# Dense weight blocks laid out by the host, and the inputs read by channels

## The chip, the cores and the metric

The kernel runs on one NeuronCore of a Trainium2 chip. The metric is the device time of one execution in microseconds. TensorE (PE) multiplies and turns, VectorE (DVE) and ScalarE (ACT) work on tiles, GpSimd (POOL) takes small powers and builds masks, SyncE (SP) issues most of the transfers (DMA). Everything is float32; a product is made of three rounded ones.

## The reference

Two transformer blocks run one after the other on x (256 tokens, 1024 channels). The first has a mixer (differential attention and a gated linear attention), cross attention to a memory `mem`, and a mixture of 32 experts of which each token takes two. The second has three attention branches, one of them cross attention to `mem_2`, gates and an output product. Every block starts with a norm over the channels and a product with a weight matrix:

```
u = rmsnorm(h) * norm_g
p = u @ w_in                       # parts: dq, dk, dv, gq, gk, gv, gg, gr
...
kv = (rmsnorm(mem) * norm_m) @ w_kv
...
kv2 = (rmsnorm(mem_2) * g_mem) @ w_mem_kv
```

The norm's row factor is one number for each token, `rsqrt(mean(x*x) + eps)`; the gain is one number for each channel.

## The kernel before

The dense products work on blocks of 1024 rows by 512 columns of weights, 40 of them, in a written order (`FIRST_BLOCKS`, 18 before the experts, `SECOND_BLOCKS`, 22 behind them). A block comes in two halves of 1 MB. `load_dense` on SP's queue loads a half into one of four buffers of the ring (`raw_half`), once the half that was there is used. From `block_cols` a half is four pieces of 512 floats, 2 KB, in each partition. ScalarE rounds the half into its hi part (`split_hi`, L898), VectorE subtracts to get the lo part in place (`split_lo`, L1418), and TensorE makes three products for each pair of tiles (`dense`, L2362 to L2364): hi by hi, hi by lo, lo by hi. With `moving` the weights stream past the inputs (512 columns a product), with `standing` the weights stand (256 columns).

The inputs must be by channels, split in the same way. x, mem and mem_2 come with tokens in partitions. ScalarE squares and sums the rows (`square_row`, `square_rows`), VectorE makes the mean, POOL the power (L784), VectorE scales the rows (`scale_rows`, L1371), TensorE turns them (`turn_normed`, 16 transposes of 128x128, L2299), and `norm_T` takes the four banks out with the gains: on ScalarE hi (L881), on VectorE lo (L1404). The same helpers serve h1, h2 and h3 later.

Each engine runs a written list in order. The lists that matter here: SP loads x, the rows of gains, gqk, gv, mem and five parameters, then dq onward. ScalarE issues six small DMAs, squares x, splits gqk's first half, takes x's hi, and goes on block by block. TensorE warms up with products nobody reads (`keep_busy`, L2320), turns the gains (`cols`), turns x, does gqk with the low-rank gates between its halves (L2439), then z (L2447), gv, dq, dk, dv, the gated attention's scores and states, the turned queries and keys, the turned memory, the heads' outputs (L2511), the first softmaxes, gg, and the memory's blocks ck0 to cv1. Mem_2 is turned between cq1 and the last turned columns of cq; its blocks are xk2 and xv2.

PSUM's eight banks are dealt by a list of uses (`PSUM_PLAN`): use n has bank n mod 8 and waits until use n - 8 is drained.

The experts' weights, 192 units of 1 MB in rows of 8 KB (L635), pass through the ring and a few other buffers. The first are loaded piece by piece as the last dense blocks of the first half release buffers; then `load_quad` refills a buffer whenever TensorE has used it. Behind the last unit (its pieces at L650) SP issues iq's first half (L611).

Of the kernel before, what the change touches and what calls it, by code (L numbers as in the profile page):

```python
# [31 lines left out]
P = 128  # L32
# [52 lines left out]
PSUM_PLAN += [f"xT{c}" for c in range(4)]  # L85
# [3 lines left out]
PSUM_PLAN += [f"memT{c}" for c in range(4)]  # L89
# [8 lines left out]
PSUM_PLAN += [f"mem2T{c}" for c in range(4)]  # L98
# [43 lines left out]
DENSE_BLOCKS = FIRST_BLOCKS + SECOND_BLOCKS  # L142
assert len(FIRST_BLOCKS) % 2 == 0
# [22 lines left out]
SCALED_ROWS = ["x", "mem", "mem2", "h2", "h3"]  # L166
# [52 lines left out]
def build(nc, A, out):  # L219
    with ExitStack() as ctx:  # L220
# [46 lines left out]
        lam_s = sb("lam_s", [P, 8])  # L267
        neg_lam = sb("neg_lam", [P, 1])
# [51 lines left out]
        d_junk = c.take(TT * H1 * DV)  # L320

# [15 lines left out]
        cq_tok, cqT = c.take(2048), c.take(2048)  # L337
        ck_tok = normed[:, :, :].rearrange("p t d -> p (t d)")
# [71 lines left out]
        mem_landed, mem2_landed = sem("mem_landed"), sem("mem2_landed")  # L410
        rows_landed, params_landed = sem("rows_landed"), sem("params_landed")
# [150 lines left out]
        W1, W2 = A["w_in"], A["w_in_2"]  # L562
        SOURCE = {"gqk": block_cols(W1, 1536), "gv": block_cols(W1, 2048), "dq": block_cols(W1, 0),
                  "dk": block_cols(W1, 512), "dv": block_cols(W1, 1024), "gg": block_cols(W1, 2560)}
        for j in range(2):
            SOURCE[f"ck{j}"] = block_cols(A["w_ckv"], 512 * j)
            SOURCE[f"cv{j}"] = block_cols(A["w_ckv"], D + 512 * j)
            SOURCE[f"wo{j}"] = block_cols(A["w_o"], 512 * j)
            SOURCE[f"cq{j}"] = block_cols(A["w_cq"], 512 * j)
            SOURCE[f"co{j}"] = block_cols(A["w_co"], 512 * j)  # L570
            SOURCE[f"out{j}"] = block_cols(A["w_out_2"], 512 * j)
        for n, b in enumerate(("mq", "mk", "mv", "mg", "dq2", "dk2", "dv2", "dg", "iq")):
            SOURCE[b] = block_cols(W2, 512 * n)
        IKW_AT = 9 * 512
        SOURCE["xq"] = block_cols(W2, IKW_AT + HD + H2)
        SOURCE["xg"] = block_cols(W2, IKW_AT + HD + H2 + 512)
        for n in range(6):
            SOURCE[f"gl{n}"] = block_cols(W2, IKW_AT + HD + H2 + 1024 + 512 * n)
        SOURCE["xk2"] = block_cols(A["w_mem_kv_2"], 0)
        SOURCE["xv2"] = block_cols(A["w_mem_kv_2"], 512)  # L580
        for n, w in enumerate(("w_up_moba_2", "w_up_dsa_2", "w_up_cross_2")):
            SOURCE[f"up{n}"] = A[w][0].rearrange("(k p) n -> p k n", p=P)
# [11 lines left out]
        def _(sp):  # L594
# [20 lines left out]
            sp.dma_start(rows[0:N_COLS, :], A["rows"]).then_inc(rows_landed, 16)  # L615
            for name in FIRST_BLOCKS[:2]:
                load_dense(name)
# [46 lines left out]
            for name in FIRST_BLOCKS[2:]:  # L664
# [8 lines left out]
                elif name == "co0":  # L673
                    wait_filled(sp, LAST_USE["cq1"])
                    load_unit(0, (1,), gate_w_of, 0, at=1)
                    wait_filled(sp, "mem2T3")
# [144 lines left out]
        def _(act):  # L821
# [99 lines left out]

            for t in range(TT):
                act.wait_ge(x_landed[t], 16)
                square_row("x", h, normed, t)
            copy("cols", cols[:, :], N_COLS)
            wait_drained(act, "cols")
            split_hi("gqk", [0])
            norm_T("x", uT_flat, "norm_mix")
# [1361 lines left out]
        def _(pe):  # L2290
# [137 lines left out]
            def gates_between(h):  # L2428
                both_drained(f"xT{2 * h}", f"xT{2 * h + 1}")
                if h == 0:  # L2430
                    return
# [704 lines left out]
```

## Time and profile before

| | us |
|---|---|
| median of 3 runs | 1029.23 (1027.38 to 1030.12) |
| the profiled execution | 1029.46 |
| its span | 1027.7 |
| TensorE busy | 855.8 |
| VectorE busy | 458.9 |
| ScalarE busy | 331.6 |
| bytes moved | 292.15 MB |

The span is the profiled part of the execution; what lies around it is 1.8 us. An engine's busy time is the sum over its instructions; a product's own span overlaps with the next one's, so starts tell more than durations.

### The profile page before, as it was taken

The page shows a single profiled execution, that of the slowest core. Times are in us where ns is not written, and L with a number is a line of the kernel's source. Part 1 is how long each engine was busy: PE and PEld are TensorE (multiplying, and loading weights), DVE is VectorE, ACT ScalarE, POOL GpSimd, SP SyncE. Part 2 cuts the span into 40 slices and gives each one's busy share as a digit, 9 for nine tenths or more (in the row PEclk, how much of TensorE's full clock was granted, in tenths as well). Part 3 has the DMA queues.
Part 4 walks back from the last instruction along what each step waited for, and adds up shares of the span by engine and source line. Part 5 has one row for each costly group of instructions (what it writes and reads, how often), then busy time and mean ns, then how long its engine had stood idle before and what let it go on. Part 6 is the DMA issues. An engine that isn't in the chain of part 4 may idle for free.

```text
span 1027.7 us, 13597 instructions
## 1 busy us (share of the span) xinstructions
PE 855.8 (83%) x5477; PEld 598.0 (58%) x5477; DVE 458.9 (45%) x853; ACT 331.6 (32%) x535; POOL 24.1 (2%) x35
## 2 busy tenths in 40 slices
PE   8999999999986475756657656766999999999997
PEld 7877888798731131212213131212788899999995
DVE  5669676674712020201102011010876788656595
ACT  4655654773320010000001000000544555455532
POOL 1030010000000000000000000000000000000000
PEclk9999999999998887978888778888999999999999
DMA  9552456496999999999999999999555454444541
GB/s 315 171 182 83 164 181 229 164 368 239 350 391 420 423 420 422 421 421 422 421 422 422 421 420 422 420 421 406 207 174 185 134 165 127 162 144 144 181 144 45
DMA packets 75711, 292.15 MB, mean 284 GB/s; under 512 B 6690, under 2 KB 7172, under 8 KB 53508
## 3 DMA queue, kind: packets, MB, share of 16 engines
q1 hardware_dynamic: 73444, 289.27, 73.1%
q10 hardware_dynamic: 2208, 2.05, 0.6%
q8 instruction: 42, 0.69, 0.3%
q14 instruction: 17, 0.14, 0.0%
HBM read 290.25 MB, written 1.05 MB: 283 GB/s over the span
## 4 chain that ended last, share of the span: by engine, by line
PE 54%; DMA 26%; SPq 9%; DVE 5%; ACT 2%; issue 1%; POOL 0%; ACTq 0%; POOLq 0%; DVEq 0%
PE bank L2362 12%; PE bank L2364 12%; PE bank L2363 11%; DMA ring<-in_w_e_gate 10%; DMA ring<-in_w_e_up 8%; DMA ring<-in_w_e_down 8%; SPq L635 7%; PE bank L2770 5%; PE bank L2299 3%; SPq L650 3%; PE bank L2789 2%; DVE ring_rounded L1418 2%; ACT ring_rounded L898 1%; DMA ring<-in_w_in 1%; PE bank L2874 1%
## 5 line engine op out<-in xcount | busy, mean ns | idle before, releaser
L1418 DVE TENSOR_TENSOR ring_rounded<-ring,ring_rounded 128x2048 fp32r<-128x2048 f32 x79 | 181.1, 2292 | 123.7 <-ACT ring_rounded L898 123.5
L898 ACT ACTIVATE ring_rounded<-ring 128x2048 fp32r<-128x2048 f32 x79 | 151.4, 1916 | 178.6 <-PE bank L2364 170.7
L2770 PE MATMUL bank<-ring,main 128*32 128x512 f32 x768 | 115.9, 759 | 74.0 <-DMA ring<-in_w_e_up 53.1
L2363 PE MATMUL bank<-ring_rounded 128*128 128x256 f32 (+1 forms) x488 | 152.4, 312 | 0.0
L2364 PE MATMUL bank<-ring_rounded 128*128 128x512 f32 x320 | 124.9, 390 | 0.0
L2770 PEld LDWEIGHTS bank<-ring,main 128*32 128x32 f32 x768 | 28.9, 134 | 151.8 <-issue 88.0
L2362 PE MATMUL bank<-uT_rounded,ring_rounded 128*128 128x256 f32 x352 | 101.8, 289 | 0.4 <-issue 0.4
L2364 PE MATMUL bank<-uT_rounded,ring_rounded 128*128 128x256 f32 x352 | 99.5, 283 | 0.0
L2789 PE MATMUL bank<-ring,main 128*32 128x512 f32 x384 | 61.3, 792 | 43.9 <-DMA ring<-in_w_e_down 43.2
L1942 DVE TENSOR_TENSOR h<-bank,h 128x512 f32<-128x512 f32 x32 | 22.0, 691 | 167.1 <-PE bank L2821 167.1
L2363 PEld LDWEIGHTS bank<-ring_rounded 128*128 128x128 f32 x488 | 93.0, 191 | 5.0
L2362 PE MATMUL bank<-ring_rounded,uT_rounded 128*128 128x512 f32 x208 | 82.7, 397 | 1.7 <-ACT main L1238 0.8
L2363 PE MATMUL bank<-ring_rounded,uT_rounded 128*128 128x512 f32 x208 | 81.0, 389 | 0.0
L2362 PEld LDWEIGHTS bank<-uT_rounded,ring_rounded 128*128 128x128 f32 x352 | 67.4, 191 | 2.3 <-issue 2.0
L2364 PEld LDWEIGHTS bank<-ring_rounded 128*128 128x128 f32 x320 | 60.0, 188 | 12.9
L2364 PEld LDWEIGHTS bank<-uT_rounded,ring_rounded 128*128 128x128 f32 x352 | 67.4, 191 | 0.0
L1927 DVE SCALAR_TENSOR_TENSOR main<-main,bank 128x512 f32<-128x512 f32 x8 | 5.5, 688 | 136.9 <-PE bank L2770 136.9
L2789 PEld LDWEIGHTS bank<-ring,main 128*32 128x32 f32 x384 | 14.1, 140 | 87.2 <-DMA ring<-in_w_e_down 51.6
L2362 PE MATMUL bank<-ring_rounded 128*128 128x512 f32 x136 | 54.2, 398 | 1.4 <-DVE ring_rounded L1404 0.9
L1161 ACT ACTIVATE main<-bank 128x512 f32<-128x512 f32 x8 | 4.8, 597 | 155.0 <-PE bank L2299 155.0
L1169 ACT ACTIVATE main<-bank 128x512 f32<-128x512 f32 x16 | 9.6, 597 | 124.7 <-PE bank L2789 124.7
L2362 PEld LDWEIGHTS bank<-ring_rounded,uT_rounded 128*128 128x128 f32 x208 | 39.0, 188 | 11.7 <-issue 2.0
(316 smaller groups left out, 1307.4 us busy)
## 6 DMA issues: line engine op xcount, KB each, us to landing
ring<-in_w_in SPq DMA_DIRECT2D x46, 1024.0 KB, 5.0
ring<-in_w_e_gate SPq DMA_DIRECT2D x44, 1024.0 KB, 26.0
ring<-in_w_e_up SPq DMA_DIRECT2D x44, 1024.0 KB, 26.3
ring<-in_w_e_down SPq DMA_DIRECT2D x36, 1024.0 KB, 26.1
main<-in_w_e_down SPq DMA_DIRECT2D x13, 1024.0 KB, 26.4
main<-in_w_e_up SPq DMA_DIRECT2D x12, 1024.0 KB, 26.4
main<-in_w_e_gate SPq DMA_DIRECT2D x12, 1024.0 KB, 26.1
ring<-in_w_ckv SPq DMA_DIRECT2D x8, 1024.0 KB, 5.1
```

The lines of the kernel that those rows point to most:

```text
L635: sp.dma_start(weight_unit(b, at + i, chunks), w_of[e, :, h * n:(h + 1) * n, :])\
L650: sp.dma_start(weight_unit(unit_buffer(p, u), i, chunks)[:, k:k + 1, at], w_of[e, :, 2 + k:3 + k, at]).then_inc(last_landed[n], 16)
L898: a.activation(rounded(hi_half(name, h)), raw_half(name, h), ACT.Copy).then_inc(hi_made, 1)
L1418: v.tensor_tensor(rounded(raw), raw, as_f32(hi_half(name, h)), ALU.subtract).then_inc(split_made, 1)
L1942: v.tensor_tensor(hs, b[:, :], hs, ALU.add).then_inc(S.added, 1)
L2299: return nc.tensor.transpose(dst, src, ident[0:k, 0:k])
L2362: mm(dst, left[0], right[0], start=first, stop=False, skip_group_check=True)
L2363: mm(dst, left[0], right[1], start=False, stop=False, skip_group_check=True)
L2364: last = mm(dst, left[1], right[0], start=False, stop=last_one, skip_group_check=True)
L2770: last = mm(bank[2 + part][on, :], xg3[:, h * (KC // 2) + k, on], weight_unit(unit_buffer(p, u), e, KC)[:, k, :], start=h + k == 0, stop=h ...
L2789: ins = mm(bank[4 + half][on, :], hidT3[:, c, on], weight_unit(unit_buffer(p, u), e, FC)[:, k, half * 512:half * 512 + 512], start=c == 0, ...
L2874: last = mm(dst, x[x_part][:, h * (KC // 2) + k, t * P:(t + 1) * P], w[w_part][:, k, :], start=h + part + k == 0, stop=h == 1 and part == ...
```

## The change

The host lays out each of the 40 dense blocks so that a partition holds its rows one behind the other; a half block is then one run of 8 KB in each partition (`blocks`, `dense_blocks`). The host also gives x, mem and mem_2 by channels (`xT`, `memT`, `mem2T`), each 1 MB more to load; x, mem and mem_2 by tokens are still loaded, for the squares (and x for the residual).

The turned inputs now hold only input times gain. Hi is made by ScalarE (`raw_hi`) and lo by VectorE (`raw_lo`), both from SBUF, without the row factor. `scale_rows` and `turn_normed` of the three inputs go. The row factor goes into what the products give: with tokens in partitions it is the scale of a copy that was there (gv, dq, dk, dv, ck, cv, xv2, the gate's tanh, the heads' norm); with tokens in the free dimension (gqk, the low-rank gates, xk2) it has to stand in a row, so VectorE scales the identity (`spread_rows`), TensorE multiplies it with ones (`row_factors`, two products), ScalarE copies it out (x_rows, mem2_rows), and VectorE multiplies by it. gqk and xk2 are drained by VectorE instead of ScalarE. gqk is computed in three passes for each half, hi by hi for all columns first. SP's first loads are now: gains, x by channels, gqk, x by tokens, gv, mem, the parameters, mem by channels. Mem_2 by channels is loaded by ScalarE's queue behind mem_2.

```diff
-PSUM_PLAN += [f"xT{c}" for c in range(4)]
+PSUM_PLAN += ["xrow0", "xrow1"]
-PSUM_PLAN += [f"memT{c}" for c in range(4)]
-PSUM_PLAN += [f"mem2T{c}" for c in range(4)]
+PSUM_PLAN += ["mrow0", "mrow1"]
...
+        SOURCE = {name: A["blocks"][n].rearrange("p (k n) -> p k n", k=FC if name in UP_BLOCKS else KC)
+                  for n, name in enumerate(DENSE_BLOCKS)}
...
+            sp.dma_start(rows[0:N_COLS, :], A["rows"]).then_inc(rows_landed, 16)
+            for j in range(2):
+                at = slice(j * 1024, (j + 1) * 1024)
+                sp.dma_start(lo_a[:, at], A["xT"][:, at]).then_inc(xT_landed[j], 16)
+            load_dense("gqk")
             for t in range(TT):
                 sp.dma_start(h[:, t, :], token_major(A["x"][0])[:, t, :]).then_inc(x_landed[t], 16)
+            load_dense("gv")
...
+            sp.dma_start(lo_b, A["memT"]).then_inc(memT_landed, 16)
...
+            def raw_hi(prefix, dst, raw, gain, chunks):
+                for c2 in chunks:
+                    for n in range(2):
+                        at = slice((2 * c2 + n) * T, (2 * c2 + n + 1) * T)
+                        last = a.activation(rounded(dst[:, at]), raw[:, at], ACT.Copy, scale=column(gain, 2 * c2 + n))
+                    last.then_inc(hi_moved, 1)
...
+            copy("cols", cols[:, :], N_COLS)
+            wait_drained(act, "cols")
+            for j in range(2):
+                act.wait_ge(xT_landed[j], 16)
+                raw_hi("x", uT_flat, lo_a, "norm_mix", (2 * j, 2 * j + 1))
+            split_hi("gqk", [0])
+            split_hi("gqk", [1])
             for t in range(TT):
                 act.wait_ge(x_landed[t], 16)
                 square_row("x", h, normed, t)
+            for t in range(TT):
+                copy(f"xrow{t}", x_rows[:, t * P:(t + 1) * P], P)
             split_hi("gv", [0])
...
+            def raw_lo(prefix, raw, hi, gain):
+                        last = v.scalar_tensor_tensor(rounded(raw[:, at]), raw[:, at], column(gain, 2 * c2 + n),
+                                                      as_f32(hi[:, at]), ALU.mult, ALU.subtract)
...
+            def spread_rows(name, spread):
+                wait_rstd(dve, name)
+                for t in range(TT):
+                    last = v.tensor_scalar(spread[:, t * P:(t + 1) * P], ident[:, :], stat(rstd, name)[:, t:t + 1],
+                                           None, ALU.mult)
+                last.then_inc(rows_spread, 1)
...
+            raw_lo("x", lo_a, uT_flat, "norm_mix")
             split_lo("gqk", [0])
...
+            split_lo("gqk", [1])
+            row_mean("x")
...
+            spread_rows("x", x_spread)
+            wait_drained(dve, "xrow1")
+            done("grT", v.tensor_tensor(grT[:, :], wait_filled(dve, "grT")[0:16, 0:T], x_rows[0:16, :], ALU.mult))
...
+            split_lo("gv", [0])
+            done("gqk0", v.scalar_tensor_tensor(two_chunks(gq), two_chunks(wait_filled(dve, "gqk0")), DA_D ** -0.5,
+                                                by_rows(x_rows), ALU.mult, ALU.mult))
+            done("gqk1", v.tensor_tensor(two_chunks(gk), two_chunks(wait_filled(dve, "gqk1")), by_rows(x_rows), ALU.mult))
+            split_lo("gv", [1])
...
-            scale_rows("mem", tiles(mix), tiles(mix))
+            row_mean("mem")
-            norm_T("mem", lo_b, memT, "norm_mem")
+            raw_lo("mem", lo_b, memT, "norm_mem")
-            scale_rows("mem2", tiles(mem2_tok), tiles(mem2_tok))
+            row_mean("mem2")
             split_lo("cq1", [1])
+            spread_rows("mem2", mem2_spread)
...
+            def row_factors(names, spread, count):
+                pe.wait_ge(rows_spread, count)
+                for t, name in enumerate(names):
+                    full(name, mm(wait_free(name)[:, 0:P], ones[:, :], spread[:, t * P:(t + 1) * P], start=True,
+                                  stop=True))
...
-            turn_normed("mem", as_tiles(mix))
-            turn_normed("mem2", as_tiles(mem2_tok))
+            row_factors(["mrow0", "mrow1"], mem2_spread, 2)
```

## Rows read from the trace of the kernel before

**Rows 1.** The page: busy tenths and GB/s in 40 slices of 25.7 us.
```profile
PE   8999999999986475756657656766999999999997
DMA  9552456496999999999999999999555454444541
GB/s 315 171 182 83 164 181 229 164 368 239 350 391 420 423 420 422 421 421 422 421 422 422 421 420 422 420 421 406 207 174 185 134 165 127 162 144 144 181 144 45
```

**Rows 2.** Waits of TensorE: for whom, us in total, times, longest.
```profile
PE bank L2770 <- DMA ring<-in_w_e_up: 53.1, 11, 6.3
```

**Rows 3.** Timeline of the start: start, duration, engine, line, operation, idle before.
```profile
2.34 0.51 ACTq L826 DMA_DIRECT2D main<-in_w_in  x1
...
6.47 1.06 ACT L851 ACTIVATE normed<-h 128x1024 f32<-128x1024 f32 x1 [4.15 <-issue]
...
6.96 0.40 PE L2299 MATMUL bank<-ident,rows 82*128 82x82 f32 x1 [0.38 <-DMA rows<-in_rows]
7.15 3.11 PE L2320 MATMUL bank<-ones,ident 128*128 128x128 f32 x20
...
10.00 1.91 ACT L898 ACTIVATE ring_rounded<-ring 128x2048 fp32r<-128x2048 f32 x1 [1.22 <-DMA ring<-in_w_in]
11.94 2.29 DVE L1418 TENSOR_TENSOR ring_rounded<-ring,ring_rounded 128x2048 fp32r<-128x2048 f32 x1 [0.72 <-ACT ring_rounded L898]
11.97 3.03 ACT L881 ACTIVATE uT_rounded<-bank,cols 128x256 fp32r<-128x256 f32 x8
...
15.90 0.36 PE L2362 MATMUL bank<-uT_rounded,ring_rounded 128*128 128x256 f32 x1 [0.43 <-issue]
...
23.46 0.23 DVE L1459 CAST causal_b<-build_m 128x128 bf16<-128x128 f32 x1 [0.74 <-POOL build_m L799]
...
30.30 1.13 PE L2447 MATMUL bank<-main 16*128 16x256 f32 x4
```

**Rows 4.** Lines L614 (x tiles) and L826 (gates): us to landing.
```profile
DMA to landing us min/median/max: 3.8/4.2/4.7
...
DMA to landing us min/median/max: 10.7/10.7/10.7
```

**Rows 5.** Windows: length, busy PE, PEld, DVE, ACT, POOL, clock, DMA share, GB/s.
```profile
0.00:25.00 25.00, 20.81 (x152) 19.70 (x153) 13.48 (x30) 12.80 (x19) 5.07 (x22) 1.00 0.93 313
...
45.00:50.00 5.00, 5.00 (x24) 4.14 (x23) 4.18 (x6) 2.45 (x3) 0.71 (x1) 1.00 0.59 184
...
230.00:240.00 10.00, 10.00 (x48) 8.51 (x47) 3.53 (x7) 3.02 (x9) 0.00 (x0) 1.00 0.51 185
...
300.00:310.00 10.00, 10.00 (x72) 5.77 (x68) 2.51 (x4) 2.36 (x4) 0.00 (x0) 1.00 1.01 421
```

**Rows 6.** Timeline of TensorE around the turned memory.
```profile
85.13 2.02 PE L2511 MATMUL bank<-main 128*128 128x128 f32 x16 [0.69 <-DVE main L1386]
...
97.28 0.55 PE L2299 MATMUL bank<-ident,main 128*128 128x128 f32 x3 [1.21 <-DVE main L1617]
```

**Rows 7.** Timeline of VectorE there.
```profile
84.91 3.22 DVE L1404 SCALAR_TENSOR_TENSOR ring_rounded<-bank,cols,ring_rounded 128x256 fp32r<-128x256 f32 x8
...
90.70 1.15 DVE L1577 TENSOR_REDUCE maxes<-bank 128x1 f32<-128x128 f32 x4
```

**Rows 8.** Timeline: a plain ScalarE copy; then TensorE and ScalarE near mem_2's transposes.
```profile
55.83 0.59 ACT L835 ACTIVATE main<-bank 128x512 f32<-128x512 f32 x1
...
204.55 2.78 PE L2299 MATMUL bank<-ident,main 128*128 128x128 f32 x24
...
205.40 0.68 ACT L835 ACTIVATE main<-bank,rstd 128x512 f32<-128x512 f32 x1
```

**Rows 9.** The critical chain behind the last expert units, and ScalarE's and TensorE's timeline.
```profile
709.38 11.72 DMA ring<-in_w_in
...
721.12 1.91 ACT L898 ACTIVATE ring_rounded<-ring 128x2048 fp32r<-128x2048 f32 x1 [0.95 <-DMA ring<-in_w_in]
...
724.55 3.70 PE L2874 MATMUL bank<-ring_rounded,uT_rounded 128*128 128x512 f32 x15 [0.39 <-ACT uT_rounded L881]
```

More of the change, by code:

```diff
@@ L560, in block_cols @@
             return w[0, :, lo:lo + width].rearrange("(k p) n -> p k n", p=P)
[L562 to L582, printed above, removed]
+        W1 = A["w_in"]
+        SOURCE = {name: A["blocks"][n].rearrange("p (k n) -> p k n", k=FC if name in UP_BLOCKS else KC)
+                  for n, name in enumerate(DENSE_BLOCKS)}
         def token_major(a):
@@ L946, in _ @@
             for t in range(TT):
-                copy(f"gv_{t}", gv[:, t * 512:t * 512 + 512])
+                copy(f"gv_{t}", gv[:, t * 512:t * 512 + 512], scale=row_of("x", t))
             split_hi("dk", [0])
@@ L964, in _ @@
             for t in range(TT):
-                copy(f"dv_{t}", dv[:, t * 512:t * 512 + 512])
+                copy(f"dv_{t}", dv[:, t * 512:t * 512 + 512], scale=row_of("x", t))
             for half in range(2):
                 copy(f"dkT{half}", dkT[:, half * 512:half * 512 + 512])
-            norm_T("mem", memT, "norm_mem")
-            wait_filled(act, "memT3")
+            act.wait_ge(memT_landed, 16)
+            wait_rstd(act, "mem")
+            raw_hi("mem", memT, lo_b, "norm_mem", range(4))
             for t in range(TT):
@@ L1130, in _ @@
             c_turned(2)
-            for half in range(2):
-                copy(f"xk2_{half}", xkT[:, half * 512:half * 512 + 512])
             co_hi(1)
@@ L1148, in _ @@
             for t in range(TT):
-                copy(f"xv2_{t}", xv2[:, t * 512:t * 512 + 512])
+                copy(f"xv2_{t}", xv2[:, t * 512:t * 512 + 512], scale=row_of("mem2", t))
             def expert_gates(S, n):
@@ L1644, in _ @@
             wait_drained(dve, "og1")
+            for t in range(TT):
+                st = rstd[:, glo + 4 * t:glo + 4 * t + 4]
+                last = v.tensor_scalar(st, st, stat(rstd, "x")[:, t:t + 1], None, ALU.mult)
+            link(last)
             mg3 = tiles(mix)[:, :, 512:1024]
@@ L3097, in in_partitions, with channel_rows, dense_blocks @@
     return w.reshape(KC, P, -1).transpose(1, 0, 2).reshape(P, -1)
+def channel_rows(x):
+    return in_partitions(np.asarray(x)[0].T)
+def dense_blocks(inputs):
+    second = 9 * 512 + HD + H2
+    at = {"gqk": ("w_in", 1536), "gv": ("w_in", 2048), "dq": ("w_in", 0), "dk": ("w_in", 512), "dv": ("w_in", 1024),
+          "gg": ("w_in", 2560), "xq": ("w_in_2", second), "xg": ("w_in_2", second + 512),
+          "xk2": ("w_mem_kv_2", 0), "xv2": ("w_mem_kv_2", 512)}
+    for j in range(2):
+        at.update({f"ck{j}": ("w_ckv", 512 * j), f"cv{j}": ("w_ckv", D + 512 * j), f"wo{j}": ("w_o", 512 * j),
+                   f"cq{j}": ("w_cq", 512 * j), f"co{j}": ("w_co", 512 * j), f"out{j}": ("w_out_2", 512 * j)})
+    at.update({b: ("w_in_2", 512 * n) for n, b in enumerate(("mq", "mk", "mv", "mg", "dq2", "dk2", "dv2", "dg", "iq"))})
+    at.update({f"gl{n}": ("w_in_2", second + 1024 + 512 * n) for n in range(6)})
+    blocks = []
+    for name in DENSE_BLOCKS:
+        if name in UP_BLOCKS:
+            w = np.asarray(inputs[UP_BLOCKS[name]])[0]
+        else:
+            w = np.asarray(inputs[at[name][0]])[0][:, at[name][1]:at[name][1] + BLOCK_COLS]
+        blocks.append(w.reshape(-1, P, w.shape[1]).transpose(1, 0, 2).reshape(P, -1))
+    return np.stack(blocks)
 def router_rows(inputs):
```

136 lines of the change are left out of this document (89 added, 47 removed).

## The prediction

> **What bounds the kernel now.** I read the 40 slices first, then the list of what TensorE waited for, then the start and the places around each changed edit engine by engine. The slices show three parts [rows 1]: TensorE is busy nine tenths to about 290 us, then the transfers take every slice at 420 GB/s to about 718 us, then TensorE is full again. The waits agree [rows 2]: the large ones are all for expert weights; between the first product and the experts TensorE waits in single places, the longest 1.21 us [rows 6]. So the front and the back are TensorE's own instruction stream, and the middle is the expert stream, whose early loads are released by TensorE's progress. A microsecond that TensorE gains before 290 us moves every release of the stream forward by the same microsecond, and the back with it. It is worth its full size if it is not eaten by VectorE or ScalarE first. The span is 1027.7 us and its execution took 1029.46 us, 0.2 over the median 1029.23; I sum against 1029.46.
>
> **1. The start.** Before, x (rows) is squared, scaled, turned on TensorE and only then split; the first product starts at 15.90, and the low-rank gates and the second half of gqk end where z starts, at 30.30 [rows 3]. After, the chain is: rows of gains land first, ScalarE ends its DMA issues at 6.4 and the turned gains are ready about 7.2 (they were turned at 6.96, waiting for their load, which was then queued behind x) [rows 3]. The channel halves of x are as large as the x tiles were and are queued behind only 41 KB, so they land about 5 to 6.3 by the x tiles' 3.8 to 4.7 us [rows 4]. The hi parts are 8 ScalarE operations on 128x256. Their form (from SBUF) isn't in the trace: below, an eighth of the 2048-wide one, 0.24; above, half of the 1024-wide square, 0.53; I take 0.37, near the same operation from PSUM (3.03 / 8) [rows 3]: 7.2 + 3.0 = 10.2. Then gqk's first half, which landed by 10.00 behind the same bytes, is split: hi 10.2 to 12.1, lo by VectorE 12.2 to 14.5 (1.91 and 2.29 us) [rows 3].
> TensorE takes the first half in three passes of 16 products, 48 in 5.7 us before (15.90 to 21.6), 1.9 each: pass one from about 12.5 (the 20 warming products end there), pass two from 14.5, pass three ends at 18.3. The low-rank gates are 24 products, 2.8 us; two small row-factor products 0.25; the second half 5.7: 27.0, where it was 30.3. **Gain 3.3 us.**
> What the new order hangs on: the gates must have landed (issued 2.34 and just behind, 10.7 us: 13.0 to 13.6 [rows 3, 4], wanted at 14.5). The row factors must be there at 21.1: x tiles now lie behind 3.2 MB; with 313 GB/s over the first 25 us [rows 5] the 4.4 MB up to their end would be in at 14.2, and since the first microseconds are slower I take 15.1, squares on ScalarE to 16.2, mean behind VectorE's second split (15.4 to 17.6), POOL's power 0.73, spread: 19.0. Two microseconds of room. gv's first half then waits on ScalarE for the factors' copies (21.8), hi 23.7, VectorE's lo behind four mask casts (three steps of 0.97 at most, POOL between [rows 3]) at 25.0 to 27.3, and is wanted at 28.1 behind z. The two scaled copies of gqk move from ScalarE to VectorE (about 0.7 each, 27.3 to 28.7), ahead of gv's second lo, whose hi is ready at 29.0 anyway. All of this is hidden; with that cover gone it would cost its 1 to 2 us. The start's bounds: 2.1 (0.53 for each hi operation) to 4.3 (0.24, and gqk landed a microsecond sooner for its longer rows).
>
> **2. The first memory.** TensorE's 16 transposes from 81.73 go; the next step (heads' outputs) began at 85.13 after a wait of 0.69 on VectorE [rows 6]. After, it needs the states, ready at 83.3, and the masked scores, earlier; its banks come free from those. It starts at 83.3, 1.8 us earlier. But the stretch to 97.28 is VectorE's: TensorE waited there 1.21 us for the softmax weights [rows 6]. VectorE's own lo parts for the memory stay at 84.9; from SBUF each costs between an eighth of the 2048-wide split, 0.29 [rows 3], and what it costs from PSUM, 3.22 / 8 = 0.40 [rows 7]; I take 0.34, so 0.5 us less. With the heads' squares 1.9 us earlier, sums, mean, the first maxima (90.70 before [rows 7]) come 1.7 earlier, the splits and exponentials with them, and the weights too: **gain 1.7 us** of the 1.8 (bounds 1.0 and 1.8). The scaling of the memory's rows (1.4 us and a 0.8 us wait for POOL on VectorE near 49) also goes, but TensorE's stall at 59.6 comes from a chain through ScalarE's exponentials and is not touched: nothing.
>
> **3. The second memory.** TensorE did 24 transposes from 204.55, 16 of them the memory's: 1.75 us. They go, two small products (0.2) come. But the eight left turn query columns whose copy on ScalarE begins at 205.40 and takes 0.68 [rows 8]. They cannot start before 206.1; they started at about 206.3. So nearly all of the 1.75 us turns into a wait on that copy: **gain 0.2** (bounds 0 and 0.4). The lo parts end at 212.0 where 212.4 was early enough for TensorE at 213.9. The scaled xk2 copies move to VectorE between two splits (1.3 us at 227; the next split's hi was ready at 228.1): nothing, at most 0.3 lost.
>
> **4. Dense blocks in 8 KB rows.** 2 KB rows give 184 GB/s at 0.59 of the engines' time, 312 per full share; the expert stream, whose rows are 8 KB, 421 at 1.01 [rows 5]. So a half block costs the engines 3.36 us now and some 2.5 after. Before 290 us and after 725 no product waits for a dense transfer [rows 2], so this is hidden, with one exception: iq's first half, issued at 709.38, lands 11.72 later, and ScalarE stood for it 0.95 us; TensorE's first product at 724.55 then waited 0.39 for ScalarE [rows 9]. It is one half block at the end of a full queue: 0.3 to 0.8 us earlier; the h3 columns it shares ScalarE with are turned until 723.3, so no more than 0.4 is usable: **gain 0.25** (bounds 0 and 0.4).
> The Trainium skill (DMA: Bandwidth & Descriptors, Specifications) asks for at least 512 B in a transfer for line rate. By that rule 2 KB rows are as good as 8 KB, this term is zero and the time 0.25 us longer. The windows of this trace don't agree (312 against 417 per full share [rows 5]), though their 2 KB stretches are bursts with gaps; the two readings differ by less than a run's scatter.
>
> **5. Scales inside copies.** A ScalarE copy with a per-partition scale takes 0.68 against 0.59 for a plain one [rows 8]: 20 or so operations, 0.1 each, all in stretches where ScalarE waits 1 to 4 us for TensorE per half block. VectorE's scaled copies cost what the copies did. The extra 1 MB loads (memory by channels) are issued beside work: nothing.
>
> **Sum.** 3.3 + 1.7 + 0.2 + 0.25 = 5.45; 1029.46 - 5.45 = 1024.0. From the bounds, gains 3.1 to 6.9: 1022.6 to 1026.4.
>
> **Rivals.**
> A. The stream gains as well. If dense loads between 200 and 270 us hold back the first expert loads, each of the 6 halves there (co and xv2) frees 0.86 us: up to 5 us more, 1019. For: the slice at 205 has the engines at nine tenths. Against: they fall to 0.51 at 230 to 240 [rows 5], so that backlog is worked off before the last releases. Chance 0.12, at some 1021.
> B. Most of the front's gain is lost to order. ScalarE's and VectorE's streams are fixed, so a late x (beyond 18.6) holds TensorE at the row factors, or the masks hold gv; and TensorE arriving earlier meets the same VectorE chains. Two microseconds at the start and one at 97: 1027. For: room of only 0.8 us at gv's lo. Against: each room above is positive. Chance 0.19.
> C. Slower: the first queue is overfilled. xT and memT put 2.1 MB more ahead of dq's first half: 10.8 MB in all. TensorE needs it landed by 34.9 (wanted at 39.1, less hi and lo). Each microsecond later costs one; from 40.3 on the whole is slower, that is below 268 GB/s over the front; at 240 it lands at 45 and the time is 1034. Against: 313 GB/s over the first 25 us with 2 KB rows [rows 5] gives 34.5, and half of the 10.8 MB comes in 8 KB rows now. Chance 0.07.
> D. The change doesn't do what it says: the scales and products are the same work elsewhere and TensorE starts no earlier, since gqk's weights land later than 12: then 1029 or so; in B's chance.
>
> **Chances.** Forecast (1022 to 1026.4) 0.62. No change means within 0.3%, 3.1 us, about what a measurement of this kernel can tell: from 1026.1 up. Faster is the forecast and A, 0.74; within is B with the weak end of C, 0.19; slower 0.07. The range 1019.5 to 1027.6 leaves out C, a little of B and of A.
>
> **What would show it.** The first product with weights near 12.5 and z near 27; heads' outputs near 80 (85.1 less the shifts of 3.3 and 1.8); a wait of about 1.3 us before the cq columns at some 200; the stream's last piece landing 5 us earlier, the back as long as before. A wait on the row factors or on gv's split, or z after 28.5, would make parts of it wrong; so would an expert stage that ends other than 5 us early.

## The result, and the profile after

The changed kernel takes 1031.87 us in the median of 13 runs (1030.89 to 1033.44), the kernel before 1029.23 on the same chip in 13 (1027.38 to 1030.77): a ratio of 1.0029, 95% interval 1.0021 to 1.0037. It is slower by about 3 us where 5.45 us of gain were forecast. The profiled execution has a span of 1029.8 us, 2.1 more than before. Bytes rise from 292.15 to 295.29 MB, the DMA packets (rows) fall from 75711 to 47103.

First the page's 40 slices: three rows, as [rows 1].

```profile
PE   6998999999996585846647566666999999999997
DMA  8653457586999999999999999999555444444541
GB/s 325 218 172 115 130 174 296 178 335 226 346 410 421 420 422 422 421 421 421 421 423 422 421 420 421 421 422 411 216 170 183 138 164 128 159 143 144 183 145 42
```

The three parts of the prediction (TensorE, then transfers, then TensorE) stand as before. What differs is the first digit of PE: 6 where [rows 1] has 8. The timeline of the start shows it (columns as in [rows 3]; L818 and L821 are the gates' and the lambdas' loads, L890 is `split_hi`, L1428 `split_lo`, L919 `raw_hi`, L2526 gqk's products, L2503 the low-rank gates', L2536 z, the small product that follows gqk).

```profile
2.34 0.44 ACTq L818 DMA_DIRECT2D main<-in_w_in  x1
...
4.09 2.19 ACTq L821 DMA_DIRECT2D main<-in_lambda_k  x1
6.31 2.37 ACTq L821 DMA_DIRECT2D main<-in_lambda_q  x1
8.71 1.10 ACTq L821 DMA_DIRECT2D main<-in_lambda_k  x1
9.86 0.24 ACT L827 ACTIVATE cols<-bank 128x82 f32<-128x82 f32 x1 [7.54 <-issue]
10.13 3.30 ACT L919 ACTIVATE uT_rounded<-ring,cols 128x256 fp32r<-128x256 f32 x8
11.18 3.25 DVE L1458 SCALAR_TENSOR_TENSOR ring_rounded<-ring,cols,uT_rounded 128x256 fp32r<-128x256 f32 x8 [8.77 <-ACT uT_rounded L919]
15.26 2.29 DVE L1428 TENSOR_TENSOR ring_rounded<-ring,ring_rounded 128x2048 fp32r<-128x2048 f32 x1 [0.83 <-ACT ring_rounded L890]
15.37 5.55 PE L2526 MATMUL bank<-uT_rounded,ring_rounded 128*128 128x256 f32 x32 [4.70 <-ACT ring_rounded L890]
...
23.53 0.23 DVE L1432 CAST main_rounded<-main 128x128 fp32r<-128x128 f32 x1 [5.97 <-DMA main<-in_gla_gate_w]
24.23 0.28 PE L2503 MATMUL bank<-uT_rounded,main_rounded 128*16 128x256 f32 x1 [1.39 <-DVE main_rounded L1433]
24.39 2.29 DVE L1428 TENSOR_TENSOR ring_rounded<-ring,ring_rounded 128x2048 fp32r<-128x2048 f32 x1
...
34.62 1.13 PE L2536 MATMUL bank<-main 16*128 16x256 f32 x4
```

Two things are late. ScalarE is not through with its DMA issues at 6.4 but at 9.8: three lambda issues that took 0.6 to 0.7 us each take 2.19, 2.37 and 1.10. And VectorE stands 5.97 us for the weights of the low-rank gates; behind that wait, in its fixed order, are gqk's second split (24.39), the mean of x and the row factors. TensorE follows: z starts at 34.62, 4.3 us later than the 30.30 of [rows 3].

The DMA view of the first 20 us has the reason. It gives, for ScalarE's queue (q10), packets, MB and share, and for a load its size and time to landing.

```profile
q1 hardware_dynamic: 1357, 6.83, 87.0%
q10 hardware_dynamic: 947, 0.06, 3.4%
main<-in_w_in ACTq DMA_DIRECT2D x1, 64.0 KB, 19.3
```

64 KB took 19.3 us to land, against 10.7 before [rows 4]. The same view of the kernel before reads:

```profile
q1 hardware_dynamic: 2582, 5.69, 82.4%
q10 hardware_dynamic: 1648, 0.21, 7.3%
```

In the same 20 us SyncE's queue moved more bytes in half as many rows, and ScalarE's queue got only 947 of its 1648 small rows through. The engines were not slack. Windows of after (columns as in [rows 5]):

```profile
5.00:10.00 5.00, 5.00 (x45) 5.00 (x45) 0.00 (x0) 0.14 (x1) 0.00 (x0) 1.00 1.03 422
15.00:20.00 5.00, 4.63 (x26) 4.66 (x27) 2.29 (x1) 4.11 (x6) 0.00 (x0) 0.66 1.03 402
```

The second row also shows a granted clock of 0.66, a mix of TensorE's two levels (1.2 and 2.4 GHz): the engine had stood idle from 10.7 to 15.4, and 32 products of gqk took 5.55 us.

Later places, TensorE and VectorE around the first memory (as [rows 6, 7]), then TensorE at the second (as [rows 8]):

```profile
87.80 2.02 PE L2599 MATMUL bank<-main 128*128 128x128 f32 x16 [1.64 <-ACT main L827]
100.33 0.55 PE L2365 MATMUL bank<-ident,main 128*128 128x128 f32 x3 [1.58 <-DVE main L1668]
```

```profile
89.20 3.25 DVE L1458 SCALAR_TENSOR_TENSOR ring_rounded<-ring,cols,ring_rounded 128x256 fp32r<-128x256 f32 x8
93.75 1.15 DVE L1628 TENSOR_REDUCE maxes<-bank 128x1 f32<-128x128 f32 x4
```

```profile
209.40 1.06 PE L2365 MATMUL bank<-ident,main 128*128 128x128 f32 x8 [1.02 <-issue]
```

And the end of the expert stream, as [rows 9]:

```profile
723.00 1.91 ACT L890 ACTIVATE ring_rounded<-ring 128x2048 fp32r<-128x2048 f32 x1 [0.74 <-DMA ring<-in_blocks]
726.61 3.72 PE L2962 MATMUL bank<-ring_rounded,uT_rounded 128*128 128x512 f32 x15 [0.36 <-ACT uT_rounded L873]
```

The starts of six steps and the span in four kernels (the last two are experiments below), in us:

| start of | before | after | gates packed | memory later |
|---|---|---|---|---|
| z | 30.3 | 34.6 | 27.2 | 27.4 |
| heads' outputs | 85.1 | 87.8 | 80.4 | 79.1 |
| turned softmax weights | 97.3 | 100.3 | 92.9 | 91.2 |
| cross scores | 207.2 | 210.3 | 202.8 | 201.2 |
| expert ranks | 269.4 | 272.8 | 265.3 | 263.7 |
| iq | 724.5 | 726.6 | 720.5 | 718.6 |
| span | 1027.7 | 1029.8 | 1023.7 | 1021.9 |

### The profile page after: what moved, and what is told of

It reads as the page before. It is cut to its first block, busy times and chain, and to the rows that moved or that the text cites. A ratio compares the mean times of both kernels' runs of the same rounds, so it can differ in the third digit from the quotient of the medians.

```text
span 1029.8 us, 13523 instructions
## 1 busy us (share of the span) xinstructions
PE 856.2 (83%) x5437; PEld 593.9 (58%) x5437; DVE 458.9 (45%) x859; ACT 333.1 (32%) x534; POOL 23.2 (2%) x35
## 2 busy tenths in 40 slices
DMA packets 47103, 295.29 MB, mean 287 GB/s; under 512 B 6754, under 2 KB 7236, under 8 KB 14404
## 3 DMA queue, kind: packets, MB, share of 16 engines
HBM read 293.40 MB, written 1.05 MB: 286 GB/s over the span
## 4 chain that ended last, share of the span: by engine, by line
PE 57%; DMA 21%; SPq 11%; DVE 6%; ACT 2%; issue 2%; POOL 0%; POOLq 0%; ACTq 0%; DVEq 0%
DMA ring<-in_w_e_down 17%; PE bank L2431 11%; PE bank L2433 11%; PE bank L2432 11%; SPq L627 9%; PE bank L2858 4%; PE bank L2877 3%; PE bank L2833 3%; DMA ring<-in_w_e_gate 2%; PE bank L2909 2%; PE bank L2365 2%; SPq L642 2%; DVE ring_rounded L1428 2%; DMA main<-in_gla_gate_w 2%; ACT ring_rounded L890 1%
## 5 line engine op out<-in xcount | busy, mean ns | idle before, releaser
L1428 DVE TENSOR_TENSOR ring_rounded<-ring,ring_rounded 128x2048 fp32r<-128x2048 f32 x79 | 181.0, 2291 | 120.1 <-ACT ring_rounded L890 119.7
L890 ACT ACTIVATE ring_rounded<-ring 128x2048 fp32r<-128x2048 f32 x79 | 151.2, 1915 | 168.9 <-PE bank L2433 158.7
L2432 PE MATMUL bank<-ring_rounded 128*128 128x256 f32 (+1 forms) x456 | 143.4, 315 | 0.0
L2431 PE MATMUL bank<-uT_rounded,ring_rounded 128*128 128x256 f32 x320 | 92.6, 289 | 0.0
L2433 PE MATMUL bank<-uT_rounded,ring_rounded 128*128 128x256 f32 x320 | 90.5, 283 | 0.0
L2432 PEld LDWEIGHTS bank<-ring_rounded 128*128 128x128 f32 x456 | 86.9, 191 | 5.0
L2433 PEld LDWEIGHTS bank<-ring_rounded 128*128 128x128 f32 x320 | 60.1, 188 | 12.9
L2431 PEld LDWEIGHTS bank<-uT_rounded,ring_rounded 128*128 128x128 f32 x320 | 61.3, 191 | 1.7 <-issue 1.4
L2433 PEld LDWEIGHTS bank<-uT_rounded,ring_rounded 128*128 128x128 f32 x320 | 61.3, 192 | 0.0
L2858 PE MATMUL bank<-main 128*32 128x512 f32 x192 | 34.9, 694 | 14.0 <-DMA uT<-in_w_e_up 14.0
## 6 DMA issues: line engine op xcount, KB each, us to landing
main<-in_w_e_down SPq DMA_DIRECT2D x13, 1024.0 KB, 27.2
```

What stands on the lines that cost most here:

```text
L890: a.activation(rounded(hi_half(name, h)), raw_half(name, h), ACT.Copy).then_inc(hi_made, 1)
L1428: v.tensor_tensor(rounded(raw), raw, as_f32(hi_half(name, h)), ALU.subtract).then_inc(split_made, 1)
L2431: mm(dst, left[0], right[0], start=first, stop=False, skip_group_check=True)
L2432: mm(dst, left[0], right[1], start=False, stop=False, skip_group_check=True)
L2433: last = mm(dst, left[1], right[0], start=False, stop=last_one, skip_group_check=True)
L2858: last = mm(bank[2 + part][on, :], xg3[:, h * (KC // 2) + k, on], weight_unit(unit_buffer(p, u), e, KC)[:, k, :], start=h + k == 0, stop=h ...
```

## The experiments

**Theory T.** The 16 DMA engines take rows of the two queues in turn. A load of many small rows in one queue therefore waits for as many rows of the other, and the wait grows with their size. The gates' columns of `w_in` are 1024 rows of 64 bytes in ScalarE's queue; the rows in SyncE's queue beside them went from 2 to 8 KB. The rivals were ScalarE's held issues, the larger amount of bytes ahead, and the new order of the start.

**1. The dose: rows of 2 and 4 KB.** Only the host's layout of the dense blocks and the view that reads it are changed (the views are shown, for 2 and for 4 KB; the three up blocks have 4 KB in the first as well).

```diff
-        SOURCE = {name: A["blocks"][n].rearrange("p (k n) -> p k n", ...)
+        SOURCE = {name: A["blocks"][n].rearrange("(k p n) -> p k n", ..., p=P)      # 2 KB
+        LOADS  = {name: A["blocks"][n].rearrange("(k p n) -> p k n", k=4, p=P)      # 4 KB: two k side by side
```

> The changed kernel with its dense blocks back in rows of 2 KB (up blocks 4 KB), everything else as changed. Theory T (turns): the engines take one row from SyncE's queue and one from ScalarE's in turn, so the 1024 rows of 64 B of the low-rank gates' weights wait for as many large rows; with 2 KB rows the gates' loads land 10 to 13 us after their issue (19.3 and 20.7 with 8 KB rows), ScalarE's six issues end by 7 (9.8), z starts at 27 to 29 (34.6) and the time is 1026 to 1028. Rival V (volume): what counts is the megabytes that SyncE issues early; they are the same, so landing stays 18 to 21 us and the time 1031 to 1033.

> As the changed kernel, dense blocks in rows of 4 KB. Theory T: landing of the gates' loads between the two others, 13 to 17 us, and the time between 1027 and 1031. Rival V: 18 to 21 us as with 8 KB.

Measured: 1026.12 us with 2 KB rows (ratio 0.9968, 0.9956 to 0.9980) and 1027.66 with 4 KB (0.9983, 0.9970 to 0.9996). The gates' loads in the DMA view of the first 20 us, at 2 KB and then at 4 KB:

```profile
main<-in_w_in ACTq DMA_DIRECT2D x1, 64.0 KB, 11.3
```

```profile
main<-in_w_in ACTq DMA_DIRECT2D x1, 64.0 KB, 15.0
```

z starts at 27.0 and 29.0. So 11.3, 15.0, 19.3 us for rows of 2, 4 and 8 KB, with everything else of the change in place: the amount of bytes ahead (rival V) is the same in all three. The DMA view of 4.5 to 13.5 us gives the rows that went through in each queue:

| | SyncE's rows | ScalarE's rows | ratio | SyncE's mean row |
|---|---|---|---|---|
| 2 KB | 1374 | 1091 | 1.26 | 2.35 KB |
| 4 KB | 930 | 718 | 1.30 | 3.77 KB |
| 8 KB | 700 | 523 | 1.34 | 5.19 KB |

For one small row about 1.3 rows of the other queue went through, whatever their size: the engines were shared by rows and not by bytes. At 2 KB VectorE waits for the gates half a microsecond:

```profile
14.39 0.23 DVE L1432 CAST main_rounded<-main 128x128 fp32r<-128x128 f32 x1 [0.51 <-DMA main<-in_gla_gate_w]
```

**2. The small rows taken away.** The host lays the gates' columns out as one row of 512 B in each partition; the dense blocks keep 8 KB.

```diff
-            act.dma_start(w_gr.rearrange("p (k n) -> p k n", k=KC), block_cols(W1, 3072, 16))
+            act.dma_start(w_gr, A["gr"])
+            "gr": lambda: in_partitions(np.asarray(inputs["w_in"])[0][:, 3072:3088]),
```

> The changed kernel with the low-rank gates' weights laid out by the host in one row of 512 B per partition: 128 rows instead of 1024, the same bytes. Theory T: they wait for an eighth of the turns and land under 8 us after issue (19.3), the lambdas' issues are no longer held up (end by 7 instead of 9.8), the first product with weights starts near 12.7 (15.37), z near 27.5 (34.6), the time 1024 to 1026. Rival V: the same 64 KB behind the same megabytes land at 17 us or later and the time is 1030 to 1032.

Measured: 1025.45 us (0.9957, 0.9944 to 0.9969). The same load, in the same view, and the start of its timeline:

```profile
q10 hardware_dynamic: 741, 0.21, 4.3%
main<-in_gr ACTq DMA_DIRECT2D x1, 64.0 KB, 7.1
```

```profile
4.85 0.49 ACTq L821 DMA_DIRECT2D main<-in_lambda_k  x1
6.40 0.24 ACT L827 ACTIVATE cols<-bank 128x82 f32<-128x82 f32 x1 [4.09 <-PE bank L2365]
11.92 4.42 PE L2526 MATMUL bank<-uT_rounded,ring_rounded 128*128 128x256 f32 x32 [1.05 <-ACT ring_rounded L890]
27.18 1.12 PE L2536 MATMUL bank<-main 16*128 16x256 f32 x4
```

The issues are back at 0.5 us each, and z starts at 27.18, where the prediction had put it (27.0). This one load of 64 KB is the whole loss at z: 7.4 us between after and this kernel. The new order of the start and the larger amount of bytes ahead are kept here, so they are not the cause.

The sizes fit T. Packing takes 896 rows out, 56 for each engine. The packed load landed after 7.1 us beside 8 KB rows and after 5.7 beside 2 KB rows (the kernel of 5); beside 4 KB it was not run, and 7.1 stands in for it. So each row taken out had cost (11.3 - 5.7) / 56 = 100 ns beside 2 KB rows, about 141 beside 4 KB, 218 beside 8 KB. At 421 GB/s [rows 5], 26 for an engine, the mean row of SyncE's queue in the table above takes 89, 143 and 197 ns. It is longer than 2 KB and shorter than 8 KB because x and x by channels, which are in that stretch too, keep 4 KB rows. The Trainium skill (DMA: Bandwidth & Descriptors, Queues, rings and completion order) says that an engine goes round the queues it has work for, a packet at a time. These numbers and the ratio of 1.3 agree with that; whether a turn holds one row of each queue or several of each, they cannot tell.

**3. The lambdas on SyncE's queue.** This frees ScalarE of the held issues, with the gates packed (`both_small`) or as they were (`lambdas_on_sp`).

```diff
-            for n, name in enumerate(("lambda_q1", ...)): act.dma_start(lam_in[...], ...)
+            for n, name in enumerate(("lambda_q1", ...)): sp.dma_start(lam_in[...], ...)   # ahead of mem
```

> The changed kernel with the four lambda loads on SyncE's queue, the gates' loads still 1024 rows of 64 B. Two waits of the change are taken apart: ScalarE is no longer held by its issues (first product near 12.5 instead of 15.37), the gates still land late (21 to 23.5). If the late landing is the whole of the 4.3 us at z, z stays at 33 to 34.6 and the time at 1030.5 to 1032; if the held issues are, z is at 28 to 30 and the time 1026 to 1028.

> As the one before, and the four lambda loads moved from ScalarE's queue to SyncE's, ahead of mem. If ScalarE's issues were held up only by the 1024 small rows ahead of them, this gives nothing more (within 1 us of the run before); if each issue waits for room of its own, ScalarE starts at 4 instead of 6.5 or later, the first product is bound by gqk's landing and lo, and the time is up to 2 us shorter.

`lambdas_on_sp`: 1031.69 us (1.0022, 1.0012 to 1.0032).

```profile
6.75 0.24 ACT L827 ACTIVATE cols<-bank 128x82 f32<-128x82 f32 x1 [4.44 <-PE bank L2365]
12.27 4.41 PE L2526 MATMUL bank<-uT_rounded,ring_rounded 128*128 128x256 f32 x32 [0.55 <-ACT ring_rounded L890]
21.47 0.23 DVE L1432 CAST main_rounded<-main 128x128 fp32r<-128x128 f32 x1 [7.02 <-DMA main<-in_gla_gate_w]
```

ScalarE is free at once, TensorE starts at 12.3, and nearly all of it is given back in front of the gates: z at 34.0, 0.7 earlier than after. So the late landing alone is enough for the loss. How much the held issues add is not shown, since a third thing came in. VectorE had the gates at 21.5, 2.1 earlier than in after, but TensorE had stood idle for 3.57 us in front of their products and did the 24 of them at a lower granted clock, in 5.1 us (22.17 to 27.25) where after took 3.0. Windows (columns as in [rows 5]):

```profile
20.00:25.00 5.00, 2.83 (x14) 1.97 (x15) 3.46 (x11) 0.00 (x0) 0.21 (x1) 0.63 0.71 269
25.00:30.00 5.00, 5.00 (x32) 4.31 (x31) 1.14 (x6) 1.96 (x3) 1.75 (x7) 0.69 0.96 384
```

What the held issues would cost with the gates in time was not run.

`both_small`: 1026.12 us (0.9965, 0.9952 to 0.9978), no gain over the packed kernel. z at 27.5, but then a new wait:

```profile
35.95 1.92 ACT L890 ACTIVATE ring_rounded<-ring 128x2048 fp32r<-128x2048 f32 x1 [3.25 <-DMA ring<-in_blocks]
```

With 512 more rows in the first queue dq's first half lands at 35.9. SyncE is held at its own issues there: it comes to dq's at 21.8 where the packed kernel does at 18.3. The prediction's rival C named 34.9 as the latest harmless time. Heads' outputs start 1.2 us later than with the gates packed alone (81.6 against 80.4), 0.35 of it from z. About a microsecond late cost about 0.9, close to what C said. In the changed kernel the point isn't reached.

**4. The layout alone, in the kernel before.** 8 KB rows are the only edit; then the same with the gates packed as in 2.

> The kernel before with one part of the change alone: all dense blocks in rows of 8 KB; inputs by rows, turned and scaled as before, the same bytes in the same order. Theory T (the engines take rows of the two queues in turn): the gates' 1024 rows of 64 B land 18 to 21 us after issue (10.7), ScalarE's six issues end near 9.8 (6.4), so x is squared 3 us later, the first product is at 19 (15.90), z at 33 to 34 (30.30), time 1031 to 1034. Rival V (more megabytes issued early): here there are no more of them, so nothing moves: 1028 to 1030.

> The kernel before, with two edits only: dense blocks in 8 KB rows, and the low-rank gates' columns of w_in laid out by the host as one row of 512 B in each partition. Theory T (the 64-byte rows of the gates' load take turns with the large rows of the other queue, and that is all the harm of the layout): gates landed by 10, ScalarE's DMA issues end before 6.5 us instead of 11.1, its first square begins at its old place (6.5), z at 30.3 give or take 0.7, ratio to before 0.9975 to 1.001. Rival L (large rows are harmful by themselves: they hold every transfer behind them, x first): x and the four lambda loads are still late, the squares begin after 9, z after 33, ratio over 1.003.

Measured: 1035.8 us alone (1.0071, 1.0054 to 1.0087), 1029.06 with packing (0.9993, 0.9984 to 1.0002). ScalarE's timeline in the first:

```profile
4.69 1.93 ACTq L812 DMA_DIRECT2D main<-in_lambda_k  x1
6.64 2.28 ACTq L812 DMA_DIRECT2D main<-in_lambda_q  x1
8.95 2.14 ACTq L812 DMA_DIRECT2D main<-in_lambda_k  x1
11.14 1.06 ACT L834 ACTIVATE normed<-h 128x1024 f32<-128x1024 f32 x1 [8.83 <-issue]
```

and in the second:

```profile
4.93 0.74 ACTq L812 DMA_DIRECT2D main<-in_lambda_k  x1
5.71 1.06 ACT L834 ACTIVATE normed<-h 128x1024 f32<-128x1024 f32 x1 [3.40 <-issue]
```

In the old order the squares of x stand behind the issues: 11.14 instead of the 6.47 of [rows 3], and z at 37.1. The loss is more than T's forecast (z at 33 to 34, at most 1034 us). The held issues are 4.7 of the 6.8 us lost at z. Most of the rest is TensorE's clock: TensorE had stood idle for 6.08 us, the granted clock from 15 to 20 us was 0.50, and its 16 transposes of x took 3.67 us instead of 1.97, the 20 warming products 3.49 instead of 2.40. The gates are not waited for (VectorE takes them at 24.5; they landed by 20.5). There the held issues are the harm; in the changed kernel, where ScalarE's first work waits for less, it is the landing. Both come from the same small rows: packed, the layout's effect can't be told from zero.

**5. Are 8 KB rows worth anything?** The changed kernel with packed gates and 2 KB rows (edits of 1 and 2 together).

> The changed kernel with the gates' columns in one row of 512 B per partition and the dense blocks back in rows of 2 KB: is a large row worth anything once it does no harm? Theory T: nothing; z at 27.0, iq's step at 720.3, 1025.4 us, within 1.0 of the kernel with packed gates and 8 KB rows. Rival W (large rows gain bandwidth where the transfers are full, at iq's first half and ahead of dq, and the packing hides that): slower than that kernel by 1.5 us or more, iq's step after 721.5. Also possible, by rows of 2 KB letting the small loads through sooner: 0.3 faster.

Measured: 1027.13 us (0.9973, 0.9964 to 0.9982), about 1.6 us slower than with 8 KB rows (0.9957), though the intervals overlap; T had said within 1.0. It meets the numbers of rival W but not its place: iq starts at 722.1, and z was already 1.5 late at 28.7; from z to iq it is 693.4 us here and 693.3 with 8 KB rows. The difference is gqk's landing. Here is its first half:

```profile
11.03 1.91 ACT L890 ACTIVATE ring_rounded<-ring 128x2048 fp32r<-128x2048 f32 x1 [1.01 <-DMA ring<-in_blocks]
```

With 8 KB rows ScalarE took it at 9.9 without a wait, with 2 KB rows and the gates unpacked at 9.7. The second half is split at 16.45, after a wait of 3.52, where 8 KB rows had it at 12.5. Longer rows don't explain this, and it may be scatter: `start_order` and `tuned` below have the same program up to z, and their traces have gqk's first half at 9.2 and 10.7, z at 26.6 and 28.0. What the windows of 10 to 14 us add is that the DMA engines were not full in the packed kernels (share 0.75 here, 0.74 with 8 KB rows, 1.09 with 2 KB rows unpacked). What left them idle stays open.

Behind z, row size is worth nothing that can be measured. The windows of 100 to 140 us say why part 4 expected more (columns as in [rows 5]; 8 KB rows, then 2 KB):

```profile
100.00:140.00 40.00, 40.00 (x206) 33.00 (x204) 27.41 (x38) 26.36 (x57) 1.64 (x1) 1.00 0.51 168
100.00:140.00 40.00, 40.00 (x210) 33.05 (x210) 26.71 (x37) 25.85 (x51) 1.64 (x1) 1.00 0.48 159
```

That is 329 and 331 GB/s per full share; from 140 to 180 us it is 371 and 355, from 230 to 240 us 349 and 338. Part 4 read 312 from a stretch of dense loads [rows 5] and put it down to their 2 KB rows. But 8 KB rows brought a few per cent at most in such stretches and didn't lift them to the stream's 417. The prediction weighed the Trainium skill's 512 B for line rate (DMA: Bandwidth & Descriptors, Specifications) against its windows and took the windows; from z on, these runs agree with the page.

**6. Order at the start.** Gates packed, fewer warming products ahead of the turned gains, gv's lo before the masks, the parameters' loads behind dq.

```diff
-            keep_busy(wait_free("xrow0"), 9)        # and 20 behind the gains
+            keep_busy(wait_free("xrow0"), 3)        # and 26
...
+            split_lo("gv", [0])                     # now ahead of the four mask casts
...
+                if name == "dq":                    # the five parameters and memT
```

> Packed gates (one row of 512 B), 3 warming products ahead of the turned gains instead of 9 (26 instead of 20 behind), gv's first lo ahead of the mask casts, parameters and mem by channels issued behind dq. With packed gates alone ScalarE stood 4.1 us for the turned gains and the first product was at 11.92, z at 27.18. If the gains are the limit, the first product comes at 11.0 to 11.3, z at 26.3 to 26.6, time 0.6 to 0.9 us under packed gates alone. Rival: gqk's landing is the limit (it was waited for in neither): nothing.

Measured: 1025.31 us (0.9967, 0.9956 to 0.9979). z comes at 26.6, as expected, but the time is no different from the packed kernel's, and z alone moves by more than this between `start_order` and `tuned`.

**7. The first memory made later.** Gates packed; the states are made ahead of gg's split, and the memory's lo parts behind the first softmax weights and ck0's split.

```diff
-            split_lo("gg", [0])
             (the states)
-            raw_lo("mem", lo_b, memT, "norm_mem")
+            split_lo("gg", [0])
...
             d_weights(1)
             split_lo("ck0", [0])
+            raw_lo("mem", lo_b, memT, "norm_mem")   # ScalarE: raw_hi behind d_pT_out(0)
```

> The changed kernel with packed gates, and the memory's lo parts moved on VectorE behind the first softmax weights and ck0's split, its hi parts on ScalarE behind the first turned weights; the gated attention's states are made ahead of gg's split. Theory V (the stretch of 80 to 100 us is VectorE's, and the 3.2 us of lo parts stood in front of it): the wait for the softmax weights shrinks from 1.6 to 0.3 or so, the cross scores begin 1.3 to 1.7 us earlier than in the kernel with packed gates (202.8), the ranks too, 1024.0 us. Rival: the time is given back at ck0, whose products then wait for the memory's parts: nothing before 202, 1025.4.

Measured: 1023.54 us (0.9939, 0.9925 to 0.9952), with 8 the fastest of the study. Its interval overlaps that of the packed kernel (0.9944 to 0.9969); the starts in the trace show where it gained. TensorE and VectorE:

```profile
79.09 2.02 PE L2598 MATMUL bank<-main 128*128 128x128 f32 x16
91.22 0.55 PE L2364 MATMUL bank<-ident,main 128*128 128x128 f32 x3 [1.20 <-DVE main L1666]
```

```profile
92.81 2.29 DVE L1428 TENSOR_TENSOR ring_rounded<-ring,ring_rounded 128x2048 fp32r<-128x2048 f32 x1
95.01 3.25 DVE L1458 SCALAR_TENSOR_TENSOR ring_rounded<-ring,cols,ring_rounded 128x256 fp32r<-128x256 f32 x8
```

The wait of 1.64 in front of the heads' outputs is gone, and the cross scores start at 201.2 against 202.8. Theory V had the size right and half of the place: the gain was made at the heads' outputs, since gg's split no longer stands before the states; the wait for the softmax weights shrank only from 1.59 to 1.20.

Both sets of edits together:

> As start_order, and the first memory's parts later: VectorE takes the states before gg's first lo, and mem's lo behind the first softmax weights (ScalarE's hi behind the first turned weights). If VectorE's order is what makes TensorE's waits of 1.6 us (heads' outputs) and 1.6 us (softmax weights), both go: 2.4 to 3.2 us under start_order, 1021 to 1022.5. Rival: the lo of mem then comes too late for ck0 (wanted some 5 us behind the weights) and gives 1 to 2 us back.

Measured: 1024.84 us (0.9956, 0.9939 to 0.9973): above the 1021 to 1022.5 that was expected, no better than the packed kernel and not the sum of the parts. From z to the cross scores it took 173.8 us where the kernel with the start's order alone took 175.7, so the memory's move worked here too; z itself came at 28.0.

**8. One load for the four lambdas**, on top of 7.

```diff
-            for n, name in enumerate(("lambda_q1", ...)): act.dma_start(lam_in[...], ...)
+            act.dma_start(lam_in[:, :], A["lam"].broadcast_to([P, 4 * DA_D]))
```

> The best kernel so far (packed gates, the memory's parts made later), and the four lambda vectors laid side by side by the host and read by one load, 128 rows of 1 KB instead of 512 rows of 256 B. Theory T (each small row of ScalarE's queue costs a turn of an engine): 384 turns fewer in the first 14 us; the rate between 10 and 14 us (275 GB/s or so with four loads) rises to 350 or more, gqk's second half and x land 0.5 to 1 us sooner, z between 26.2 and 27.2 instead of 27.4, time 1022.5 to 1023.5, ratio to before 0.993 to 0.994. Rival: z is set by gqk's first half and ScalarE's and VectorE's splits, which stand by then; z within 0.3 of 27.4, no change of time.

Measured: 1023.51 us (0.9941, 0.9927 to 0.9955). Windows of this kernel and of 7's:

```profile
10.00:14.00 4.00, 2.95 (x25) 2.68 (x23) 3.18 (x4) 3.25 (x3) 0.00 (x0) 1.00 0.89 315
```

```profile
10.00:14.00 4.00, 2.94 (x25) 2.78 (x25) 3.17 (x5) 3.80 (x3) 0.00 (x0) 1.00 0.73 244
```

384 small rows fewer raise the rate from 244 to 315 GB/s, less than T's 350, and z moves by 0.2 us: the rival was right. Most of the rise is the engines' share, 0.73 to 0.89, and not faster turns: per full share it is 334 and 354 GB/s. T has no account of engines that stand idle.

## Why the prediction was wrong

**The step that failed** is in part 1: "the gates must have landed (issued 2.34 and just behind, 10.7 us: 13.0 to 13.6 [rows 3, 4], wanted at 14.5)". It landed at 21.6 to 23.5. The 10.7 us were read from a trace in which the other queue held 2 KB rows, and were carried over into one where part 4 had made these rows four times as long. The prediction even had the number of small rows within reach (64 KB in pieces of 16 floats) and treated the landing as bytes behind bytes. The same error is in "ScalarE ends its DMA issues at 6.4": beside 8 KB rows its queue drained one small row for 1.3 large ones, and its issues took 1.1 to 2.4 us; with the gates packed they took 0.4 to 0.6. In place of 10.7 us the runs show 11.3, 15.0 and 19.3 for rows of 2, 4 and 8 KB in the other queue, and 7.1 for the packed load. With 0.9 us of room ahead of 4 more steps, this was the place to bound from both sides, and no rival stood for it: C, the slower one, looked at the first queue's bytes, B stopped at 1027 and D at 1029.

**Part 1 otherwise held.** With the gates packed z came at 27.18 for 27.0, the row factors' spread was done at 19.3 for 19.0, the first product at 11.9 for 12.5. A hi operation from SBUF took 3.30 / 8 = 0.41 us, for 0.37.

**Part 2** (gain 1.7). From z to the heads' outputs after needs 53.18 us where before needed 54.83: 1.65 gained. At the turned softmax weights 1.27 are left. The lo parts cost 3.25 / 8 = 0.41, not 0.34: an operand in SBUF brought nothing over one in PSUM (0.40 [rows 7]), and that is the missing 0.4. They began at 89.2, which is the forecast's 84.9 moved by z's 4.3.

**Part 3** (gain 0.2): from there to the cross scores, 109.97 after and 109.89 before, nothing. The wait came in the described place, 1.02 us for 1.3; the trace puts it to issue, and ScalarE's copy had ended 0.1 us before. **Part 4** (gain 0.25): ScalarE's wait for iq's half went from 0.95 to 0.74, TensorE's from 0.39 to 0.36: 0.03 used. Its 2.5 us for a half block in 8 KB rows rested on the reading of the windows that experiment 5 doesn't bear out. **Part 5** (nothing): from the cross scores to the ranks 0.29 us were lost; where was not looked into.

**The sum that came**: -4.32 (z) + 1.65 - 0.38 - 0.08 - 0.29 = -3.4 at the ranks. From the ranks to iq it was 453.8 us, 1.4 less than before; over the twelve experiments it was 454.7 to 455.7, those with late gates among them. So this is probably the scatter of one execution and not the change; the medians are 2.6 to 3 us apart. Rival A's gain in the stream never came: with the gates packed the ranks are 4.1 us early and iq is 4.1.

**The forecast's total** of 5.45 would have been 4.0 with the failed step mended (span 1023.7, ratio 0.9957): 0.2 lost at z, 0.4 in the first memory, 0.2 at the second, 0.3 from there to the ranks, 0.3 at iq. The inputs by channels are worth about 3 to 4 us (0.9973, 0.9968 and 0.9957 where the gates are in time); the 8 KB layout with the gates unpacked takes away 6 to 7 (1.0071 alone; 1031.87 against 1025.45, or 1.0029 against 0.9957, here).

## What to carry to other kernels

A transfer's time to landing belonged to the two queues together: when rows in one queue grew, the load of many small rows in the other took longer with them, though no byte was added. So before making rows longer, list the strided loads that are in flight beside them (count their rows, not their bytes), and let the host pack those first. An engine that issues such loads can be held at its own next issue; moving the others away helped little here as long as the small rows stayed. And compare a transfer rate only with one from the same kind of stretch: the rate of a long full stretch is no promise for bursts.

## What the runs showed of the hardware

- A load of 64 KB in 1024 rows landed after 11.3, 15.0 and 19.3 us beside rows of 2, 4 and 8 KB, and after 7.1 us as 128 rows.
- Over 9 us the engines took 1.26 to 1.34 rows of SyncE's queue for one row of ScalarE's, with dense rows of 2 to 8 KB in the first and mostly rows of 64 B in the second.
- ScalarE's DMA issues took 0.4 to 0.7 us with the gates packed and 1.1 to 2.4 us with 1024 small rows draining beside 8 KB rows (one of 1.47 in a packed kernel, `tuned`). SyncE's issues were held too, up to 3.2 us each with the gates packed.
- Dense loads in bursts moved 329, 371 and 349 GB/s per full share in 8 KB rows, 331, 355 and 338 in 2 KB rows (three stretches).
- ScalarE's copy of 128x256 with a scale from SBUF took 0.41 us where the one from PSUM took 0.38 [rows 3]; VectorE's subtraction 0.41 and 0.40 [rows 7].
- TensorE idle from 10.7 to 15.4 came back at a granted clock of 0.66 over the next 5 us: 32 products in 5.55 us, against 4.42 where the idle time was 1.05. After 3.57 us of idle time 24 products took 5.1 us against 3.0 (0.63 and 0.69), after 6.08 us 16 transposes 3.67 against 1.97 (0.50).
